# Products with few output rows, dealt out over four groups of 32 output partitions, in a four-layer hybrid trunk

## The chip, the cores and the metric

The kernel runs as one program on 1 core of one Trainium2 chip. The metric is the device time of one execution in microseconds; lower is better. The number compared is the median over several runs.

## The reference, cut to what matters

One inference step of a trunk with four layers of kinds A, B, C, A, on 128 context tokens and 256 latent tokens, model width D = 1024, all in fp32. Each layer first makes its modulation vectors from two conditioning vectors, and its mixer follows. Three parts of it matter here:

```
sc, scc = silu(c), silu(c_ctx)                      # two vectors of 1024
for l in range(4):                                  # kinds A, B, C, A
    mod_p = scc @ w_mod[l] + b_mod[l]               # 1024 x 3072 weights, one row each:
    mod_s = sc  @ w_mod[l] + b_mod[l]               #   two "modulation rows" per layer
    h = rmsnorm(y) * (1 + scale) + shift            # from mod, per sequence
    ...
# kind A (layers 0 and 3): input and forget gates of 4 heads in 2 directions = 16 rows
    gin  = concat([q, k, v])                        # q, k, v: 4x4 blocks of xc, xc, xm (2048 wide)
    ipre = gin @ w_ig + b_ig ;  lf = log_sigmoid(gin @ w_fg + b_fg)
# kind B (layer 1): decay through rank 16, two directions
    la[d] = log_sigmoid((h @ w_a1[d]) @ w_a2[d] + b_a[d]) / 16
```

## The kernel before, in words

Every engine has one instruction list, written out by hand, and the lists meet in semaphores. Activations lie with features on the partitions: `hT` is 8 blocks of 128 features by 385 columns (128 context tokens, a spare column, 256 latent tokens). Nearly every product writes one of two PSUM banks, `acc0` and `acc1`, in a fixed order of tiles that `plan()` numbers. TensorE may write tile n when tile n-2 has been moved out (`acc_moved`), and the mover, mostly ScalarE, waits for `acc_ready`.

All big weights stream through a `ring` of two slots of 2 MB, filled by the SP queue in a fixed order of chunks. A chunk's DMAs are issued when the last tile that reads the chunk two places earlier is done.

**Modulation.** A layer's 3072 modulation columns are made in `MOD_CHUNKS` = 8 parts of `MC` = 384. One part (`mod_part`) is one ring chunk of 1.5 MB and one group of `KD` = 8 products: the stationary operand is a pair of columns of `sc` (the two silu vectors, 128 features of them), the moving one is 128 x 384 of the weights, and the output is 2 x 384. ScalarE moves this to `mst`. `mod_columns` then turns it into columns with three transposes of 2 x 128, and ScalarE moves 6 columns to `modr`. Layer 0's parts run at the start, between the four `fold` steps, which build gate weights on VectorE. The parts of layer l+1 run inside layer l: two per head in layer 0 (`head`: one between the score products and `den`, the other before the products with the state), six between the levels of layer 1's attention and two after it, and one after every second head of layer 2. Layer 3 runs none.

**Gate sums.** In `mlstm` (layers 0 and 3), 32 products with 16 stationary columns (`g4`, in `gfold`, which lies in `kw[0]`) and 385 moving columns sum up into a 16 x 385 tile: 16 of them on `xm`, then 16 on `xc`. ScalarE moves that to `grow`, and two products with the selector `gsel` spread the 16 rows to rows 0 to 3 and 32 to 35 of two tiles.

**The low-rank step.** In `gla` (layer 1), two groups of 8 products with 16 stationary columns (`ga1`), one per direction, write 16 x 385 each. ScalarE moves both to `gha`, and 8 products with `ga2` (16 rows of contraction) follow. GpSimd's queue loads `ga1`, `ga2` and the layer's state when the layer begins.

Each product appears once in the kernel and twice in the trace: the program issues 8 products for a modulation part, and the trace has 16 matmul records, each with its own weight load, in the order in which the products stand.

Of the kernel before, what the change touches and what calls it, by code (L numbers as in the profile page):

```python
# [55 lines left out]
CHUNK = 4096  # L56

# [3 lines left out]
def plan():  # L61
# [12 lines left out]
    for l, kind in enumerate(KINDS):  # L74
        folds = [[(name, l, *counts) for name, *counts in part] for part in fold]
        if l == 0:
            phases += mod(0, 0, 1) + folds[0] + folds[1] + mod(0, 2, 3) + folds[2] + mod(0, 4, 5) + folds[3]
            phases += mod(0, 6, 7) + folds[4]
        phases += [("norm", l, 0, 2)]
        if kind == 0:  # L80
            if l:
                phases += sum(folds, [])
            phases += [("xm", l, 4, 16), ("z", l, 4, 16), ("gate", l, 0, 3), ("pre", l, 0, 12), ("cols", l, 0, 1)]
            for h in range(AH):
                first, second = mod(l + 1, 2 * h), mod(l + 1, 2 * h + 1)

                phases += [(f"first{h}", l, 0, 1)] + first + [(f"c0_{h}", l, 1, 0), (f"state{h}", l, 0, 9)] + second
                phases += [(f"rest{h}", l, 0, 14 if h < AH - 1 else 2)]
            phases += [("out", l, 4, 8)]
        elif kind == 1:  # L90
            phases += [("q", l, 1, 4), ("k", l, 1, 4), ("la", l, 0, 10), ("v", l, 2, 6), ("g", l, 2, 8)]
            phases += [("state", l, 0, 6)] + mod(l + 1, 0, 1, 2, 3, 4, 5) + [("rms", l, 0, 3)] + mod(l + 1, 6, 7)
            phases += [("rms3", l, 0, 1), ("out", l, 2, 8)]
        else:
            phases += [("q", l, 2, 8), ("k", l, 2, 8), ("rmsq", l, 0, 8), ("v", l, 2, 6), ("rmsk", l, 0, 8),
                       ("g", l, 2, 8), ("turn", l, 0, 2), ("knew", l, 0, 2)]
            for k in range(KD):
                phases += [(f"attn{k}", l, 0, 1)] + mod(l + 1, k)
            phases += [("out", l, 2, 8)]
    phases += [("store", 0, 0, 6)]  # L100
    for name, l, chunks, tiles in phases:
        if name in ("xm", "z", "v", "g", "out") or name in ("q", "k") and KINDS[l] == 2:
            assert c % 2 == 0 and t % 2 == 0
# [13 lines left out]
def trunk(nc, i, o):  # L117

    with ExitStack() as ctx:
# [45 lines left out]
        with ExitStack() as st:  # L165
# [7 lines left out]
            kw = [sb(f"kw{d}", ADH, stack=st) for d in range(2)]  # L173
# [31 lines left out]
        g4 = gfold.rearrange("p (f s n) -> p f s n", s=2, n=16)  # L205
# [7 lines left out]
        with ExitStack() as st:  # L213
# [17 lines left out]
            ga2 = sb("ga2", 2 * BH * BDK, rows=RANK, stack=st)  # L231
            gha = sb("gha", 2 * W, rows=RANK, stack=st)
# [38 lines left out]
        const_dve = sem("const_dve")  # L271
        ring_full = [sem(f"ring_full{s}") for s in range(SLOTS)]
# [219 lines left out]
        def _(pe):  # L492
# [88 lines left out]

            def mod_columns(l, n):
                t = tile(f"modrow{n}", l)
                moved(pe, t)
                transposes(tile(f"modcol{n}", l), [
                    (lambda ps, e=e: ps[:, 2 * e:2 * e + 2], mst[:, seg(n % 2 * MC + e * P, P)])
                    for e in range(MC // P)])

            def mod_part(l, n):


                if l == DEPTH:
# [5 lines left out]
                group(ps[0:2, 0:MC], [(sc[:, 2 * k:2 * k + 2], w3[:, k, :]) for k in range(KD)]  # L598
                      ).then_inc(acc_ready, 1)
# [153 lines left out]
            def mlstm(l):  # L753
# [37 lines left out]
            def gla(l):  # L791
# [3 lines left out]
                pe.wait_ge(b_in, 16 * 5)  # L795
# [3 lines left out]
                for d in range(2):  # L799
                    moved(pe, tile("la", l, d))  # L800
                    for h in range(BH):
                        n = d * BH + h
                        mm(bank(tile("la", l, 2 + n))[:, 0:W], ga2[:, n * BDK:(n + 1) * BDK],
                           gha[:, d * W:(d + 1) * W], True, True).then_inc(acc_ready, 1)
# [171 lines left out]
        def _(act):  # L976
# [42 lines left out]
            move(tile("vec", 0, 1), sc.rearrange("p (k r) -> p r k", r=2),  # L1019
# [13 lines left out]
            def mod_part(l, n):  # L1033
# [3 lines left out]
                move(tile(f"modrow{n}", l), mst[:, seg(n % 2 * MC, MC)], lambda ps: ps[0:2, 0:MC])  # L1037
# [83 lines left out]
            def mlstm(l):  # L1121
# [16 lines left out]
                nc.scalar.copy(grow[:, 0:P], ps[0:16, 0:P])  # L1138
                move(tile("gate", l, 0), grow[:, P:TC], lambda ps: ps[0:16, LAT:W])
# [33 lines left out]
            def gla(l):  # L1173
# [4 lines left out]
                for d in range(2):  # L1178
                    move(tile("la", l, d), gha[:, d * W:(d + 1) * W], lambda ps: ps[0:RANK, 0:W])
                for n in range(2 * BH):  # L1180
                    both_sequences(tile("la", l, 2 + n), dx[0][:, n * TC:(n + 1) * TC], bias=vec[:, V_BA + n:V_BA + n + 1])
                moved_all(act, "la", l, 10)
# [127 lines left out]
        def _(dve):  # L1310
# [11 lines left out]
            for t, x in ((vrow[:, :], 0.0), (rowp[:, :], 0.0), (eps[:, :], EPS), (ones[:, :], 1.0),  # L1322
                         (ones_d[:, :], 1.0 / D), (ones_h[:, :], 1.0 / ADH),
                         (y3[:, :, NCTX:LAT], 0.0)):
                ins = nc.vector.memset(t, x)
            ins.then_inc(const_dve, 1)

# [48 lines left out]
            def prepare(l):  # L1376

                done_before(dve, l - 1)
                for t in (xm3[:, :, 0:1], xm3[:, :, W + 1:W + 2], gsel, r_ab[:, :], r_m[:, :]):
                    ins = nc.vector.memset(t, 0.0)  # L1380
                link(ins)
                dve.wait_ge(const_made, CONSTS)
                for x in range(4):
# [4 lines left out]
                nc.vector.tensor_copy(gsel.rearrange("p (n c) -> p n c", c=32)[:, :, 0:AH],  # L1388
                                      ident[0:16, 0:16].rearrange("p (n c) -> p n c", c=AH)).then_inc(gsel_ready, 1)
# [320 lines left out]
        def _(pool):  # L1710
# [57 lines left out]
            def gla(l):  # L1768
                done_before(pool, l - 1)
                for d in range(2):  # L1770
                    pool.dma_start(ga14[:, :, d, :], i["b_w_a1"][0, d].rearrange("(k p) n -> p k n", p=P)).then_inc(b_in, 16)
                    pool.dma_start(ga2[:, seg(d * BH * BDK, BH * BDK)], i["b_w_a2"][0, d]).then_inc(b_in, 16)
# [90 lines left out]
```

## Time and profile before

| what | value |
|---|---|
| time of 3 runs, median (lowest, highest) | 1951.1 us (1944.92, 1952.26) |
| the profiled execution: its own time, first to last instruction | 1948.8 us |
| TensorE busy | 1816.9 us, 93% |
| VectorE, ScalarE, GpSimd busy | 604.2, 495.2, 167.7 us |
| mean granted TensorE clock | 0.968 of 2.4 GHz |
| share of the chain that ended last that is TensorE's | 88% |

Shares are of the span. A line that begins with L500 is the helper `mm` that issues every plain product, and one that begins with L565 is a transpose, so groups are told apart by their tiles (`acc<-ring,sc` is the modulation rows). A matmul's busy time runs from its start to the modelled end, and neighbours overlap: 16 records of 0.486 us each can take 5.32 us together.

### The profile page before, as it was taken

The numbers are of one execution on the slowest core, as the hardware profiler recorded it, in microseconds if no ns is written. First come the engines' busy times: TensorE is split into PE (matmuls) and PEld (weight loads), VectorE is DVE, ScalarE is ACT, GpSimd is POOL, SyncE is SP. The second block draws the span as 40 slices with busy tenths as digits, with TensorE's granted clock in tenths as the row PEclk, the third lists the DMA queues.
The fourth block names the chain that finished last, engine by engine and source line by source line (L and its number), as shares of the span: only waits on it lengthen the run. The fifth ranks groups of instructions, "written<-read, shape, count | busy, mean of one in ns | idle before, by whom it ended". The sixth has DMA issues, their size and how long they took to land.

```text
span 1948.8 us, 16614 instructions
## 1 busy us (share of the span) xinstructions
PE 1816.9 (93%) x6421; PEld 1050.9 (54%) x6421; DVE 604.2 (31%) x979; ACT 495.2 (25%) x960; POOL 167.7 (9%) x158
## 2 busy tenths in 40 slices
PE   6899999999989899988989998999799998898998
PEld 3355534755655554546455455545455536575655
DVE  0333005336340202375320552321433005445420
ACT  2201323323320114343111222231201223433300
POOL 1000001001000000052043000000100001100100
PEclk9999998999999998999999997999899999999999
DMA  6522222233242321242365221323222221212122
GB/s 189 203 86 86 88 74 76 76 112 116 83 146 95 113 86 43 76 150 98 130 126 156 86 86 44 98 98 110 73 86 87 99 74 44 83 48 87 44 88 75
DMA packets 105140, 185.98 MB, mean 95 GB/s; under 512 B 5136, under 2 KB 54704, under 8 KB 105072
## 3 DMA queue, kind: packets, MB, share of 16 engines
q1 hardware_dynamic: 95816, 158.40, 24.2%
q0 software_dynamic: 8640, 26.46, 4.6%
q8 instruction: 49, 0.80, 0.2%
q10 hardware_dynamic: 616, 0.16, 0.1%
q14 instruction: 19, 0.16, 0.0%
HBM read 164.47 MB, written 20.54 MB: 95 GB/s over the span
## 4 chain that ended last, share of the span: by engine, by line
PE 88%; DVE 5%; ACT 3%; issue 1%; DMA 1%; SPq 0%; DVEq 0%; ACTq 0%; POOLq 0%
PE acc L500 69%; PE mix L500 17%; PE acc L565 1%; DMA out_new_C<-cst 1%; DVE hT L1523 1%; ACT cp L1276 1%; DVE mix L1344 1%; DVE rd L1505 1%; DVE cstat L1666 1%; PE mix L915 0%; DMA ring<-in_a_w_out 0%; DMA cst<-in_c_k_g 0%; DVE dx L1590 0%; DVE hT L1348 0%; DVE fqk L1626 0%
## 5 line engine op out<-in xcount | busy, mean ns | idle before, releaser
L500 PE MATMUL acc<-hT,ring 128*128 128x385 f32 x1664 | 548.3, 491 | 15.8 <-DVE hT L1351 14.4
L500 PEld LDWEIGHTS acc<-hT,ring 128*128 128x128 f32 x1664 | 317.9, 192 | 244.6 <-issue 21.9
L500 PE MATMUL acc<-z,ring 128*128 128x385 f32 x512 | 169.5, 492 | 6.1 <-DMA ring<-in_a_w_out 4.2
L500 PE MATMUL acc<-ring,sc 128*2 128x384 f32 x512 | 170.2, 486 | 1.6 <-ACT mst L992 1.2
L500 PEld LDWEIGHTS acc<-z,ring 128*128 128x128 f32 x512 | 97.9, 192 | 77.7 <-issue 6.1
L500 PE MATMUL mix<-qs,ring 128*128 128x256 f32 x512 | 117.6, 392 | 9.6 <-DVE qs L1507 9.6
L500 PEld LDWEIGHTS mix<-qs,ring 128*128 128x128 f32 x512 | 100.1, 197 | 27.6 <-issue 13.2
L500 PEld LDWEIGHTS acc<-ring,sc 128*2 128x2 f32 x512 | 41.3, 85 | 119.1 <-issue 112.2
L1363 DVE SCALAR_TENSOR_TENSOR y<-acc,modv,y 128x128 f32 x64 | 23.4, 413 | 223.8 <-PE acc L500 223.8
L500 PE MATMUL acc<-ring,hT 128*128 128x512 f32 x192 | 85.5, 608 | 0.0
L500 PE MATMUL acc<-xc,bd 128*128 128x385 f32 x128 | 57.5, 574 | 14.2 <-DVE hT L1523 8.4
L500 PE MATMUL acc<-vtok,kw 128*128 128x512 f32 x128 | 61.5, 610 | 5.9 <-ACT cst L992 5.9
L1445 DVE SCALAR_TENSOR_TENSOR pm<-pm,fl 64x384 f32<-64x384 f32 x2 | 1.1, 550 | 207.3 <-ACT fl L1145 207.3
L500 PEld LDWEIGHTS acc<-ring,hT 128*128 128x128 f32 x192 | 37.3, 195 | 48.1 <-issue 48.1
L992 ACT ACTIVATE mst<-acc 2x384 f32<-2x384 f32 x32 | 15.3, 479 | 177.4 <-PE acc L500 177.4
L1523 DVE TENSOR_TENSOR hT<-hT,acc 128x385 f32<-128x385 f32 x32 | 15.6, 551 | 137.5 <-PE acc L500 137.5
L1123 ACT COPY xm<-acc 128x385 f32 x32 | 15.4, 480 | 163.1 <-PE acc L500 163.1
L1757 POOL TENSOR_SCALAR kw<-ktok,cols 128x512 f32<-128x512 f32 x16 | 34.3, 2150 | 250.4 <-ACT ktok L992 238.1
L1047 ACT ACTIVATE hT<-y x24 | 12.6, 525 | 167.6 <-DVE y L1363 167.2
L992 ACT ACTIVATE cst<-acc 128x512 f32<-128x512 f32 x64 | 37.7, 597 | 68.4 <-PE acc L500 55.8
L500 PE MATMUL acc<-hT,ones_h 128*128 128x385 f32 x128 | 44.7, 491 | 9.1 <-ACT hT L1118 9.1
L1666 DVE TENSOR_REDUCE cstat<-mix 128x1 f32<-128x384 f32 (+1 forms) x48 | 19.5, 462 | 98.4 <-PE mix L500 98.4
(297 smaller groups left out, 2212.6 us busy)
## 6 DMA issues: line engine op xcount, KB each, us to landing
ring<-in_w_mod SPq DMA_DIRECT2D x64, 768.0 KB, 6.2
ring<-in_a_w_in SPq DMA_DIRECT2D x32, 1024.0 KB, 6.9
ring<-in_state_mlstm_C SPq DMA_DIRECT2D x16, 1024.0 KB, 7.8
out_new_C<-cst POOLq DMA_DIRECT2D x32, 512.0 KB, 3.2
ring<-in_a_w_out SPq DMA_DIRECT2D x16, 1024.0 KB, 7.8
ring<-in_c_w_in SPq DMA_DIRECT2D x16, 1024.0 KB, 7.6
ring<-in_b_w_in SPq DMA_DIRECT2D x12, 1024.0 KB, 6.3
ring<-in_b_w_out SPq DMA_DIRECT2D x4, 1024.0 KB, 6.2
```

Source lines behind the costliest of these rows:

```text
L500: return nc.tensor.matmul(out, lhsT=lhsT, rhs=rhs, start=start, stop=stop)
L565: ins = nc.tensor.transpose(out(ps), src, ident[0:src.shape[0], 0:src.shape[0]])
L992: nc.scalar.activation(out, src(ready(n)), func, **kw_).then_inc(acc_moved[n % 2], 1)
L1047: nc.scalar.activation(hT[:, bass.ds(it * (2 * W) + e * W, W)], y[:, bass.ds(it * (2 * W) + e * W, W)], ACT.Square).then_inc(sq_ready, 1)
L1123: pair_loop(tile("xm", l), AT_, lambda it, e, ps: nc.scalar.copy(xm[:, bass.ds(it * (2 * (W + 2)) + (e * (W + 2) + 1), W)], ps[:, 0:W]))
L1276: ins = nc.scalar.activation(cp[s][:, seg(c, n)], mix[:, seg(q * 512, n)], ACT.Exp, bias=cst_[s][:, q:q + 1], accum_out=cst_[s][:, 3 + q:4 ...
L1344: link(nc.vector.reciprocal(inv, rstd[:, :]))
L1363: ins = stt(yc, ps[:, seg(c, n)], modv[:, bass.ds(it * 4 + (2 * (2 * KD + e) + r), 1)], yc, ALU.mult, ALU.add)
L1505: link(nc.vector.reciprocal(rd[d][:, :], rd[d][:, :]))
L1523: tt(h3[:, e, :], h3[:, e, :], acc[t % 2][:, 0:W], ALU.subtract).then_inc(cen_ready if e < HT - 1 else acc_moved[t % 2], 1)
L1666: ins = nc.vector.tensor_reduce(st_[:, q:q + 1], mix[:, seg(q * 512, n)], AX, ALU.max)
L1757: nc.gpsimd.tensor_scalar(kw[d][:, :], ktok[:, :], cols[:, seg(192 + 32 * d + h, 1)], None, ALU.mult).then_inc(kw_ready, 1)
```

## The change

Every group of products with 2 or 16 output rows now goes to four groups of 32 output partitions. Product n writes partitions 32j to 32j+31 with j = n mod 4, so four partial sums stand in one bank, and the products that follow add them.

- The modulation products take 32 columns of `sc` in place of 2: the pair, and 30 of the columns behind it, whose rows nobody reads. `mst` has 128 rows. `mod_columns` has three full products with a selector `sel` (128 x 2, a one in row p and column r where p mod 32 = r) in place of three transposes.
- The gate products take 32 columns of `gfold` (16 of them zero); `gfold` is cleared each time and lies in both halves of `kw`, `gsel` and `grow` in `qs`, and `gsel` has its rows four times.
- The low-rank step takes both directions at once (32 columns): 8 products in place of 16 and one move in place of two. `ga2` is cleared on GpSimd and loaded four times over, in 8 DMAs in place of 2.

```diff
-        sc = sb("sc", 2 * KD)
+        sc = sb("sc", 2 * KD + GRP - 2)
+        sel = sb("sel", 2)
-        mst = sb("mst", 2 * MC, rows=2)
+        mst = sb("mst", 2 * MC)
-        gfold = kw[0]
-        grow = kw[1][0:16, 0:TC]
+        gfold = kw_both
+        grow = qs[0][:, 0:TC]
+            def packed(ps, width, n, a, b, first, last):
+
+                j = n % NG
+                return mm(ps[j * GRP:(j + 1) * GRP, 0:width], a, b, first, last)
...
-                transposes(tile(f"modcol{n}", l), [
-                    (lambda ps, e=e: ps[:, 2 * e:2 * e + 2], mst[:, seg(n % 2 * MC + e * P, P)])
-                    for e in range(MC // P)])
+                for e in range(MC // P):
+                    ins = mm(ps[:, 2 * e:2 * e + 2], mst[:, seg(n % 2 * MC + e * P, P)], sel[:, :], True, True)
+                ins.then_inc(acc_ready, 1)
...
-                group(ps[0:2, 0:MC], [(sc[:, 2 * k:2 * k + 2], w3[:, k, :]) for k in range(KD)]
-                      ).then_inc(acc_ready, 1)
+                for k in range(KD):
+                    ins = packed(ps, MC, k, sc[:, 2 * k:2 * k + GRP], w3[:, k, :], k < NG, k >= KD - NG)
+                ins.then_inc(acc_ready, 1)
...
-                    ins = mm(ps[0:16, 0:W], a, b, n == 0, n == len(pairs) - 1)
+                    ins = packed(ps, W, n, a, b, n < NG, n >= len(pairs) - NG)
...
-                for d in range(2):
-                    group(bank(tile("la", l, d))[0:RANK, 0:W], [(ga14[:, k, d, :], h3[:, k, :]) for k in range(KD)]
-                          ).then_inc(acc_ready, 1)
+                for k in range(KD):
+                    ins = packed(ps, W, k, ga1[:, k * GRP:(k + 1) * GRP], h3[:, k, :], k < NG, k >= KD - NG)
...
-                for t in (xm3[:, :, 0:1], xm3[:, :, W + 1:W + 2], gsel, r_ab[:, :], r_m[:, :]):
+                for t in (xm3[:, :, 0:1], xm3[:, :, W + 1:W + 2], gsel, gfold, r_ab[:, :], r_m[:, :]):
...
+                nc.gpsimd.memset(ga2[:, :], 0.0).then_inc(ga2_zero, 1)
...
+                    for g in range(NG):
+                        pool.dma_start(ga2[seg(g * GRP + d * RANK, RANK), seg(d * BH * BDK, BH * BDK)], i["b_w_a2"][0, d]
+                                       ).then_inc(b_in, 16)
```

On TensorE, around layer 0's gate sums (`acc<-xm,kw` and `acc<-xc,kw`), the list before reads:

```order
L500 MATMUL acc<-xm,kw 16x385 x16
L500 MATMUL acc<-xc,kw 16x385 x16
L500 MATMUL acc<-kw 64x384 x2
L500 MATMUL acc<-xc,bd 128x385 x8
L500 MATMUL acc<-bd,xm 128x128 x12
```

And now:

```order
L506 MATMUL acc<-xm,kw 32x385 x16
L506 MATMUL acc<-xc,kw 32x385 x16
L506 MATMUL acc<-qs 64x384 x2
L506 MATMUL acc<-xc,bd 128x385 x8
L506 MATMUL acc<-bd,xm 128x128 x12
```

Nothing moved: the counts are the same, the outputs have 32 rows, and the selector is read from `qs`.

On TensorE, in layer 0's first head, from the products for the denominators' first part (`acc<-aq,vec`) to the products with the stored state (`mix<-qs,ring`), before:

```order
L500 MATMUL acc<-aq,vec 128x256 x8
L500 MATMUL acc<-ring,sc 2x384 x8
L500 MATMUL mix<-pm,ones 128x128
L500 MATMUL mix<-pm,ones 128x256 x2
L500 MATMUL mix<-pm,ones 128x128
L500 MATMUL mix<-pm,ones 128x256 x2
L500 MATMUL acc<-vtok,kw 128x512 x8
L500 MATMUL acc<-ktok,cols 2x512
L500 MATMUL acc<-ring,sc 2x384 x8
L565 MATMUL acc<-ident,mst 128x2 x3
L500 MATMUL mix<-qs,ring 128x256 x32
```

And now:

```order
L506 MATMUL acc<-aq,vec 128x256 x8
L506 MATMUL acc<-ring,sc 32x384 x8
L506 MATMUL mix<-pm,ones 128x128
L506 MATMUL mix<-pm,ones 128x256 x2
L506 MATMUL mix<-pm,ones 128x128
L506 MATMUL mix<-pm,ones 128x256 x2
L506 MATMUL acc<-vtok,kw 128x512 x8
L506 MATMUL acc<-ktok,cols 2x512
L506 MATMUL acc<-ring,sc 32x384 x8
L506 MATMUL acc<-sel,mst 128x2 x3
L506 MATMUL mix<-qs,ring 128x256 x32
```

Again nothing moved: the modulation products write 32 rows, and the three transposes have become three products.

On GpSimd, the loads at the start of layer 1 (`ga` is both `ga1` and `ga2`), before:

```order
L1771 DMA ga<-in_b_w_a 128x8x16
L1772 DMA ga<-in_b_w_a 16x512
L1771 DMA ga<-in_b_w_a 128x8x16
L1772 DMA ga<-in_b_w_a 16x512
L1773 DMA gs<-in_state_gla_S 128x8x256
L1774 IOTA gxor 128x128
L1775 IOTA gxs 128x128
```

And now:

```order
L1789 MEMSET ga 128x1024
L1791 DMA ga<-in_b_w_a 128x8x16 x2
L1795 DMA ga<-in_b_w_a 16x512 x8
L1797 DMA gs<-in_state_gla_S 128x8x256
L1798 IOTA gxor 128x128
L1799 IOTA gxs 128x128
```

The memset and six more DMAs stand ahead of the state's DMA and of the two iotas.

## Rows read from the trace of the kernel before

**Rows 1.** The page: span, busy time by engine, the last chain by engine.

```profile
span 1948.8 us, 16614 instructions
PE 1816.9 (93%) x6421; PEld 1050.9 (54%) x6421; DVE 604.2 (31%) x979; ACT 495.2 (25%) x960; POOL 167.7 (9%) x158
...
PE 88%; DVE 5%; ACT 3%; issue 1%; DMA 1%; SPq 0%; DVEq 0%; ACTq 0%; POOLq 0%
```

**Rows 2.** TensorE's groups by shape: count, busy us, mean ns, idle us ahead.

```profile
L500 PE MATMUL acc<-ring,sc 128*2 128x384 f32 x512 | 170.2, 486 | 1.6 <-ACT mst L992 1.2 <-DVE rd L1401 0.4
...
L500 PE MATMUL acc<-xc,kw 128*16 128x385 f32 x64 | 21.1, 486 | 0.0
L500 PE MATMUL acc<-xm,kw 128*16 128x385 f32 x64 | 21.1, 487 | 0.0
...
L500 PE MATMUL acc<-hT,ga 128*16 128x385 f32 x32 | 10.5, 486 | 0.0
```

**Rows 3.** Timeline of TensorE, layer 0's first head: start us, length us.

```profile
297.24 3.00 PE L500 MATMUL acc<-bd,xm 128*128 128x128 f32 x24
...
318.20 5.32 PE L500 MATMUL acc<-ring,sc 128*2 128x384 f32 x16
323.45 2.44 PE L500 MATMUL mix<-pm,ones 128*128 128x128 f32 x12
...
340.80 0.34 PE L565 MATMUL acc<-ident,mst 2*128 2x2 f32 x3
```

**Rows 4.** The tile mst: its transposes, min, median and max ns.

```profile
L565 PE MATMUL acc<-ident,mst x96: 189/196/219, 31.0 to 1337.1; 2*128 2x2 f32 x96
```

**Rows 5.** Timeline of TensorE at the start, layer 0's modulation parts.

```profile
39.75 5.43 PE L500 MATMUL acc<-ring,sc 128*2 128x384 f32 x16
...
45.74 5.32 PE L500 MATMUL acc<-ring,sc 128*2 128x384 f32 x16 [0.30 <-ACT mst L992]
...
83.05 5.49 PE L500 MATMUL acc<-hT,ones_d 128*128 128x256 f32 x32 [1.19 <-issue]
```

**Rows 6.** DMA from 20 to 80 us: rate in 40 slices, us to landing.

```profile
GB/s 5 0 0 0 25 230 401 372 143 363 400 163 0 11 0 0 0 45 315 398 290 34 321 399 290 5 29 229 397 384 38 217 397 376 30 0 164 404 388 396
...
ring<-in_w_mod SPq DMA_DIRECT2D x12, 768.0 KB, 5.6
```

**Rows 7.** Timeline of VectorE in layer 0's first head, ahead of the denominators.

```profile
318.31 0.75 DVE L1483 TENSOR_TENSOR rd<-wi,acc 128x256 f32<-128x256 f32 x2 [7.54 <-PE acc L500]
...
320.24 0.41 DVE L1489 TENSOR_TENSOR pm<-pm,mix 128x256 f32<-128x256 f32 x1
```

**Rows 8.** Layer 1's level loop, 841 to 905 us: each engine's busy us, PEclk.

```profile
841.00:905.00 64.00, 55.94 (x306) 30.87 (x304) 53.72 (x26) 24.56 (x37) 34.49 (x7) 1.00 0.51 164
```

**Rows 9.** The same loop: the chain that ended last.

```profile
873.80 5.25 PE acc L500 x16
...
882.20 5.25 PE acc L500 x16
...
887.73 1.49 issue
889.22 2.92 PE mix L500 x24
```

**Rows 10.** The same loop: timelines of ScalarE and GpSimd.

```profile
887.49 0.48 ACT L992 ACTIVATE mst<-acc 2x384 f32<-2x384 f32 x1 [4.63 <-PE acc L500]
...
882.94 6.17 POOL L1784 TENSOR_TENSOR fqk<-fqk,gk 128x1536 f32<-128x1536 f32 x1 [5.59 <-ACT fqk L1211]
```

**Rows 11.** Layer 2, one modulation part: timelines of TensorE and ScalarE.

```profile
1213.90 5.32 PE L500 MATMUL acc<-ring,sc 128*2 128x384 f32 x16
1219.15 0.92 PE L500 MATMUL mix<-ck,cq 64*128 64x128 f32 x4
...
1214.27 0.20 ACT L1276 ACTIVATION_READ_ACCUMULATOR cp<-mix,cstat 128x1 f32 x1
```

**Rows 12.** Layer 1's start: timelines of GpSimd and TensorE.

```profile
671.47 0.90 POOL L1773 DMA_DIRECT2D gs<-in_state_gla_S  x1
...
722.08 10.54 PE L500 MATMUL acc<-hT,ga 128*16 128x385 f32 x32
```

**Rows 13.** A memset's length, and TensorE's wait in layer 3's fold.

```profile
0.97 0.48 DVE L1325 MEMSET cst<- 128x512 f32 x1 [0.97 <-PEq L1852]
...
1397.94 5.13 PE L500 MATMUL acc<-z 128*128 128x256 f32 x12 [1.92 <-DVE z L1384]
```

More of the change, by code:

```diff
@@ L56 @@
 CHUNK = 4096
+GRP = 32
+NG = P // GRP
 def plan():
@@ L102, in plan @@
         if name in ("xm", "z", "v", "g", "out") or name in ("q", "k") and KINDS[l] == 2:
-            assert c % 2 == 0 and t % 2 == 0
+            assert c % 2 == 0
         chunk0[name, l], tile0[name, l] = c, t
@@ L172, in trunk @@
             ktok = sb("ktok", ADH, stack=st)
-            kw = [sb(f"kw{d}", ADH, stack=st) for d in range(2)]
+            kw_both = sb("kw", 2 * ADH, stack=st)
             bd = sb("bd", 3 * HT * P, stack=st)
@@ L191, in trunk @@
         nst = r_ab[0:2, 0:ADH]
-        gfold = kw[0]
-        grow = kw[1][0:16, 0:TC]
-        gsel = kw[1][0:16, TC:TC + P]
+        kw = [kw_both[:, d * ADH:(d + 1) * ADH] for d in range(2)]
+        gfold = kw_both
+        grow = qs[0][:, 0:TC]
+        gsel = qs[0][:, TC:TC + P]
         vrow = cst[0][:, 0:4 * P]
@@ L204, in trunk @@
         bd4 = bd.rearrange("p (m e c) -> p m e c", m=3, e=HT)
-        g4 = gfold.rearrange("p (f s n) -> p f s n", s=2, n=16)
+        g4 = gfold.rearrange("p (f s n) -> p f s n", s=2, n=GRP)
         qs3 = [v3(t, HT, NLAT) for t in qs]
@@ L793, in gla @@
                 linear("k", l, 1, KD, 4, h3, W)
-                pe.wait_ge(b_in, 16 * 5)
-                for d in range(2):
-                    group(bank(tile("la", l, d))[0:RANK, 0:W], [(ga14[:, k, d, :], h3[:, k, :]) for k in range(KD)]
-                          ).then_inc(acc_ready, 1)
[L799 to L804, printed above, removed]
+                pe.wait_ge(b_in, 16 * 11)
+                ps = bank(tile("la", l, 0))
+                for k in range(KD):
+                    ins = packed(ps, W, k, ga1[:, k * GRP:(k + 1) * GRP], h3[:, k, :], k < NG, k >= KD - NG)
+                ins.then_inc(acc_ready, 1)
+                moved(pe, tile("la", l, 0))
+                for n in range(2 * BH):
+                    mm(bank(tile("la", l, 1 + n))[:, 0:W], ga2[:, n * BDK:(n + 1) * BDK], gha[:, :], True, True
+                       ).then_inc(acc_ready, 1)
                 linear("v", l, 2, KD, 4, h3, W, tokens=True)
@@ L1036, in mod_part @@
                     return
-                move(tile(f"modrow{n}", l), mst[:, seg(n % 2 * MC, MC)], lambda ps: ps[0:2, 0:MC])
+                move(tile(f"modrow{n}", l), mst[:, seg(n % 2 * MC, MC)], lambda ps: ps[:, 0:MC])
                 for m in range(max(n - 1, 0), n + (n == MOD_CHUNKS - 1)):
@@ L1137, in mlstm @@
                 ps = ready(tile("gate", l, 0))
-                nc.scalar.copy(grow[:, 0:P], ps[0:16, 0:P])
-                move(tile("gate", l, 0), grow[:, P:TC], lambda ps: ps[0:16, LAT:W])
+                nc.scalar.copy(grow[:, 0:P], ps[:, 0:P])
+                move(tile("gate", l, 0), grow[:, P:TC], lambda ps: ps[:, LAT:W])
                 move(tile("gate", l, 1), r_ig, lambda ps: ps[0:64, 0:TC], ACT.Identity, bias=rowp[:, ia:ia + 1])
@@ L1177, in gla @@
                     both_sequences(tile("k", l, h), gk3[:, h, :])
-                for d in range(2):
-                    move(tile("la", l, d), gha[:, d * W:(d + 1) * W], lambda ps: ps[0:RANK, 0:W])
+                move(tile("la", l, 0), gha[:, :], lambda ps: ps[:, 0:W])
                 for n in range(2 * BH):
-                    both_sequences(tile("la", l, 2 + n), dx[0][:, n * TC:(n + 1) * TC], bias=vec[:, V_BA + n:V_BA + n + 1])
-                moved_all(act, "la", l, 10)
+                    both_sequences(tile("la", l, 1 + n), dx[0][:, n * TC:(n + 1) * TC], bias=vec[:, V_BA + n:V_BA + n + 1])
+                moved_all(act, "la", l, 9)
                 link(nc.scalar.activation(dx[1][:, :], dx[0][:, :], ACT.Abs))
@@ L1323, in _ @@
                          (ones_d[:, :], 1.0 / D), (ones_h[:, :], 1.0 / ADH),
-                         (y3[:, :, NCTX:LAT], 0.0)):
+                         (y3[:, :, NCTX:LAT], 0.0), (sc[:, :], 0.0)):
                 ins = nc.vector.memset(t, x)
             ins.then_inc(const_dve, 1)
+            dve.wait_ge(const_made, CONSTS)
+            nc.vector.tensor_reduce(sel[:, :], ident.rearrange("p (j r) -> p r j", r=GRP)[:, 0:2, :], AX, ALU.add
+                                    ).then_inc(sel_ready, 1)
             def mod_vectors(l):
```

28 lines of the change are left out of this document (18 added, 10 removed).

## The prediction

> **What bounds the kernel now.** I read the page first: TensorE is busy 93% of a span of 1948.8 us, and 88% of the chain that ended last is TensorE's [rows 1]. So a product that gets shorter counts nearly in full, unless it covers somebody else's work. Then the groups by shape, for what the change touches: the modulation rows take 170.2 us (512 records, 32 parts of 16), the gate sums 21.1 + 21.1 us over two layers, the low-rank step's first half 10.5 us [rows 2]. That is 222.9 us. The reader should see that the mean of one record is 486 or 487 ns in all four groups, whether 2 or 16 output rows are written, and that 16 of them take 5.32 us [rows 3]. So records start (5.32 - 0.486)/15 = 0.322 us apart: the 384 or 385 moving columns set the pace, and the output rows don't. Last I read the places where modulation parts stand between other engines' work: the start, the heads, the level loop of layer 1, and layer 2.
>
> **The dealt groups.** The program keeps the same number of products (16 fewer records in the low-rank step). Whether products for different groups of 32 output rows run at the same time is the whole question, and no row before shows two groups side by side. If they don't, a record still starts 0.322 us after the last; if four do, four start in that time. What I take lies between, for this reason: a product is two records, both for the same rows, and records stand in the trace in the order of the list. The second record of a product needs the rows that the first still streams through, so it starts 0.322 us later; the next product's first record stands behind it in the list, and can start with it, not before. So two run at a time, and n products take n steps and the last record's 0.486 us.
>
> The Trainium skill (TensorE: Matmul & The Clock Gate, Part 3, The mechanism) says that matmuls start and end in program order, and that weight loads alone are pulled ahead. By that rule the two at a time stand, and with them the sum below. The same part of that page (Measured speedup vs the span model) has three column tiles of 32 at 2.38 times; by that alone a part would take 5.32/2.38 = 2.24 us and the kernel, by the same sum, about 1845 us, which is an estimate from that page; no run here shows such tiles yet.
>
> A step is 0.322 us plus the time d between two starts that don't wait for each other. d lies between 0 and the closest starts I find, the three transposes: 0.34 us in all, the last 0.196, so (0.34 - 0.196)/2 = 0.072 us apart [rows 3, 4]. I take 0.03, under the middle, as a transpose's start also loads 128 stationary columns, and these load 32.
>
> **A modulation part**: 8 x 0.352 + 0.486 = 3.30 us in place of 5.32, a gain of 2.02. Against it, three products with `sel` replace three transposes of 0.34 us. They have 128 stationary columns and 2 moving ones and are six records; 24 records of 128 by 128 take 3.00 us [rows 3], 0.12 apart, so six take about 0.72: a loss of 0.38, between 0 (as before) and 0.54 (0.12 x 5 + a full record of 0.278). Net 1.64 us a part.
>
> Of the 32 parts, 26 stand where TensorE has no other wait to fall back on, if their covers hold:
> - Layer 0's eight, at the start. Six parts and other work lie between 39.75 and 83.05 us [rows 5]; 6 x 5.66 are parts, 9.3 the rest. After: 6 x 4.02 + 9.3 = 33.4 us, 5.6 a chunk. A chunk of 1.57 MB takes 3.9 us at the 400 GB/s that the rate reaches, and 5.6 us from issue to landing [rows 6]. That is just hidden.
> - Eight in layer 0's heads. The first part of a head covers VectorE's scaling of the scores: that ends at 320.24 + 0.41 = 320.65 [rows 7], 2.45 us after the part's start [rows 3]. 3.30 us still cover it. Behind the second part only shared shifts follow.
> - Eight in layer 2. The part covers the exponentials that the next scores wait for; they end at 1214.47, 0.57 us into it [rows 11].
> - Two after layer 1's attention, with nothing beside them.
>
> 26 x 1.64 = 42.6 us.
>
> The other six stand in layer 1's level loop, and there VectorE is busy for 53.7 of 64 us, nearly as long as TensorE [rows 8]. In the loop's second half the last chain does run through parts [rows 9], because ScalarE waits for a part's end before it makes the next factors, and GpSimd's 6.17 us product follows those [rows 10]. A shorter part brings that forward until VectorE or GpSimd is late instead, which the "issue" piece of 1.49 us already shows. Three parts on the chain would give 4.9 us; I take 3.5, between 1 and 4.9.
>
> **Gate sums**: 32 x 0.352 + 0.486 = 11.75 us a layer, 23.5 for both in place of 42.2: 18.7 us. What waits for them (ScalarE, then VectorE's rows) moves forward with them.
>
> **Low-rank step**: 8 products in place of 16, so 3.30 in place of 10.54 us: 7.2 us. Its loads grow by a memset and six DMAs ahead of the state's. The state's DMA was issued at 671.47, each issue takes at most 0.9 us, and the step starts at 722.08 [rows 12]; with ten more microseconds of queue (six issues and the memset) and a landing like that of a ring chunk (5.6 us, [rows 6]), over 30 us are left. So nothing; if the cover were gone, some 10 us.
>
> **Clearing `gfold`**: 128 x 1024, twice the 0.48 us of a 128 x 512 memset [rows 13]. In layer 0 it runs while TensorE makes the first two parts, ahead of any fold product. In layer 3 TensorE waits for the VectorE copies right behind it [rows 13], so 1.0 us is lost.
>
> **Sum**: 42.6 + 3.5 + 18.7 + 7.2 - 1.0 = 71.0 us. 1948.8 - 71.0 = 1877.8. The runs shown have a median of 1951.1, 2.3 us over the profiled span, so I add that: **1880 us**. With d = 0, the columns at no loss and the loop at 4.9 this case gives 58.8 + 4.9 + 20.6 + 7.5 - 1.0 = 90.8, so 1860; with d = 0.072, the columns at 0.54 and the loop at 1 it gives 29.6 + 1 + 16.0 + 6.9 - 1.0 = 52.5, so 1899.
>
> **Rivals.**
>
> *Four at a time.* The second record of a product doesn't hold up the next product. For it: nothing in a row forbids it. Against it: in all rows records start in list order. A part then takes 3 x 0.322 + 0.486, about 1.5 us, net 3.44, but covers give out: at the start six chunks need 23.4 us of DMA against 22.6 us of work, and the landing shows too (3.5 us in all); each head's first part leaves 1.0 us of VectorE's 2.45 open (4 us). 26 x 3.44 - 7.5 = 82; loop 4.9; gates 42.2 - 2 x 5.3 = 31.6; low rank 9.0; less 1.0: 126.5, so **1825 us**. The Trainium skill (TensorEngine Tiling, Theoretical Speedup) allows up to 4 times for 32 columns.
>
> *No overlap at all*, so the change doesn't do what it says: the step stays 0.322 us whatever the rows. For it: one pace for 2 and for 16 rows [rows 2]. Then the selector products cost 26 x 0.38 = 9.9 and 1 in the loop, the memset 1.0, and the low-rank step still halves (-5.2): +6.7, so **1958 us**.
>
> *Slower.* A change of group makes a record wait until the one before is written out: 0.486 between starts and not 0.322, 0.164 more. That falls on 7 changes a part and 31 in a gate sum: 26 x (1.15 + 0.38) + 5.5 in the loop + 2 x 5.1 - 4.1 + 1.0 = 52, so **2003 us**. It decides early: with no overlap, 0.012 us a change (251 changes) is enough for 0.5% slower. The Trainium skill (TensorEngine Tiling, Key Properties) says that changing the tiling mode drains the array, and not changing the tile; by that rule this rival's price is not paid. No row here shows a change of group.
>
> **Chances.** Two at a time 0.58, four 0.20, no overlap 0.12, slower 0.10. About 0.5% (10 us) is what a measurement of this kernel can tell from no change. So faster 0.78, same 0.12, slower 0.10. The likeliest case has 1860 to 1899 by itself; with four at a time the range is 1818 to 1900, and the other two are left out.
>
> **What would show it.** In the changed trace, 16 `acc<-ring,sc` records in about 3.3 us, starting in twos about 0.35 us apart, each still 0.48 us long; the gate's 64 in 11.8; six `acc<-sel,mst` records in 0.7; TensorE waiting on nothing new at the start; VectorE as busy as before in layer 1's loop, now without TensorE beside it. It is wrong if the records run one or four at a time, if the parts' covers were thinner than I read them, or if TensorE's granted clock, 1.00 in that loop now [rows 8], falls to 1.2 GHz there once TensorE pauses between levels: a level's products of 2.92 us [rows 9] and a part would then take some 13 us together, and the loop would give back up to 24 us.

## The result, and the profile after

The changed kernel takes 1830.54 us (median of 4 runs, 1827.67 to 1837.2), beside 1951.27 us before (4 runs, 1944.92 to 1952.26): a ratio of 0.9395, 95% interval 0.9371 to 0.942, so 121 us less. The forecast was 1880 us, with 1818 to 1900 as the range. The time lies inside the range, but not where the likeliest case had it (1860 to 1899): the case of four at a time, which had a chance of 0.20, gave 1825.

The page of the changed kernel, with the span, TensorE's share and the last chain's shares, answers to [rows 1]:

```profile
span 1825.9 us, 16809 instructions
PE 1672.0 (92%) x6501; PEld 1033.8 (57%) x6501; DVE 608.4 (33%) x989; ACT 497.9 (27%) x959; POOL 172.1 (9%) x165
...
PE 84%; DVE 7%; ACT 3%; DMA 3%; issue 2%; ACTq 0%; SPq 0%; DVEq 0%; POOLq 0%
```

TensorE still bounds the kernel. What shrank is seen in its groups by shape, against [rows 2]:

```profile
L506 PE MATMUL acc<-ring,sc 128*32 128x384 f32 x512 | 49.6, 506 | 5.3 <-DMA ring<-in_w_mod 5.3
...
L506 PE MATMUL acc<-xm,kw 128*32 128x385 f32 x64 | 5.6, 490 | 0.0
L506 PE MATMUL acc<-xc,kw 128*32 128x385 f32 x64 | 5.5, 487 | 0.0
...
L506 PE MATMUL acc<-hT,ga 128*32 128x385 f32 x16 | 1.5, 493 | 0.0
```

The mean of one record is as before (486 to 506 ns), and the counts of the first three groups too. But 170.2 us became 49.6, and 42.2 became 11.1: the records of different groups lie on top of one another. How many at a time is read from the timeline of TensorE's products (start, length, count) at layer 0's gate sum and in its first head:

```profile
241.45 2.79 PE L506 MATMUL acc<-xm,kw 128*32 128x385 f32 x32
244.06 2.77 PE L506 MATMUL acc<-xc,kw 128*32 128x385 f32 x32
...
281.06 1.50 PE L506 MATMUL acc<-ring,sc 128*32 128x384 f32 x16
282.77 2.44 PE L506 MATMUL mix<-pm,ones 128*128 128x128 f32 x12 [0.21 <-DVE pm L1508]
```

and from that of its weight loads in the same part:

```profile
281.06 0.16 PEld L506 LDWEIGHTS acc<-ring,sc 128*32 128x32 f32 x8 [0.33 <-issue]
281.41 0.13 PEld L506 LDWEIGHTS acc<-ring,sc 128*32 128x32 f32 x4 [0.19 <-issue]
...
```

A part of 16 records takes 1.50 us where it took 5.32 [rows 3]: four rounds of four records each, 0.322 to 0.35 us apart. The loads show it plainly: eight at once (for each of the four groups the first record and, behind it, its second), then four with each round. The 64 records of a gate sum go the same way, 5.4 us in all.

Where the 122.9 us between the two profiled executions lie, from the starts of TensorE's first record of each stage in the two timelines (us; the differences are taken before rounding):

| stage | before | after | difference | forecast |
|---|---|---|---|---|
| start, to layer 0's norm (8 parts) | 83.0 | 61.7 | -21.3 | -13.1 |
| two gate sums | 43.2 | 12.2 | -30.9 | -18.7 |
| layer 0's heads to the low-rank step (8 parts) | 414.6 | 386.9 | -27.7 | -13.1 |
| low-rank step | 19.2 | 9.2 | -10.1 | -7.2 |
| layer 1's `v` and `g` to its loop | 98.0 | 94.9 | -3.1 | 0 |
| level loop (6 parts) | 68.2 | 65.6 | -2.6 | -3.5 |
| loop's end to `out` (2 parts) | 35.9 | 31.7 | -4.2 | -3.3 |
| layer 2 (8 parts) | 394.4 | 370.1 | -24.3 | -13.1 |
| layer 3's norm to its gate sum (`gfold` cleared) | 195.1 | 196.2 | +1.2 | +1.0 |
| all else | 597.3 | 597.4 | +0.2 | 0 |

A part outside the loop gains 3.82 us, and its columns (the products with `sel`) lose some 0.42: from their start to that of the next product it is 0.69 us in the first head (296.27 to 296.96), where it was 0.27 (340.80 to 341.07). That is 3.40 net. 26 of them would be 88.4; the four stages with parts show 77.5. The view of TensorE's waits names most of the rest, three waits for ring chunks that weren't there before, 5.3 + 2.1 + 1.7 = 9.1 us:

```profile
PE acc L506 <- DMA ring<-in_w_mod: 5.3, 3, 2.7
...
PE acc L506 <- DMA ring<-in_c_w_out: 2.1, 1, 2.1
PE acc L506 <- DMA ring<-in_b_w_out: 1.7, 1, 1.7
```

They stand where longer parts covered a transfer; for the two `out` weights this is read from the place alone, and no run tried it. At the start (timeline, against [rows 5]) the parts wait for their own weights:

```profile
41.76 1.50 PE L506 MATMUL acc<-ring,sc 128*32 128x384 f32 x16 [2.75 <-DMA ring<-in_w_mod]
...
45.94 1.81 PE L506 MATMUL acc<-ring,sc 128*32 128x384 f32 x16 [1.92 <-DMA ring<-in_w_mod]
...
61.72 5.49 PE L506 MATMUL acc<-hT,ones_d 128*128 128x256 f32 x32 [1.19 <-issue]
```

Behind the second of these waits a part takes 1.81 us and not 1.50: from 20 to 62 us the granted clock has a mean of 0.84, where before it had 0.96. In a second trace of the changed kernel (`e9_after_again`) the clock is 0.92 there, the three waits of 5.3 us are four of 7.3, and the norm starts at 60.87.

The level loop hardly moved, though TensorE lost most of six parts there. A level's products need two factors: VectorE makes one (its `fqk` product) and GpSimd the other. The loop's window of 64 us (busy us of each engine, then the granted clock), and VectorE's, GpSimd's and TensorE's timelines in it, against [rows 8 to 10]:

```profile
763.20:827.20 64.00, 41.54 (x321) 34.22 (x320) 55.88 (x27) 25.43 (x37) 35.19 (x7) 0.82 0.50 165
```

```profile
767.92 4.99 DVE L1645 TENSOR_TENSOR fqk<-fqk,gq 128x1536 f32<-128x1536 f32 x1
...
786.26 1.75 DVE L1645 TENSOR_TENSOR fqk<-fqk,gq 128x1536 f32<-128x1536 f32 x1
```

```profile
766.63 4.66 POOL L1808 TENSOR_TENSOR fqk<-fqk,gk 128x1536 f32<-128x1536 f32 x1 [7.05 <-ACT fqk L1224]
...
783.45 7.87 POOL L1808 TENSOR_TENSOR fqk<-fqk,gk 128x1536 f32<-128x1536 f32 x1 [7.23 <-ACT fqk L1224]
...
801.79 7.91 POOL L1808 TENSOR_TENSOR fqk<-fqk,gk 128x1536 f32<-128x1536 f32 x1 [5.55 <-ACT fqk L1224]
```

```profile
761.47 4.63 PE L506 MATMUL mix<-fqk 128*128 128x128 f32 x40
...
772.97 5.07 PE L506 MATMUL mix<-fqk 128*128 128x128 f32 x24 [5.44 <-DVE fqk L1645]
...
781.22 2.94 PE L506 MATMUL mix<-fqk 128*128 128x128 f32 x24 [1.00 <-DVE fqk L1645]
...
791.41 4.39 PE L506 MATMUL mix<-fqk 128*128 128x128 f32 x24 [5.06 <-issue]
...
809.80 5.39 PE L506 MATMUL mix<-fqk 128*128 128x128 f32 x24 [5.10 <-issue]
...
827.12 2.05 PE L506 MATMUL mix<-dx,gs 128*128 128x256 f32 x4 [4.28 <-DVE dx L1652]
```

VectorE is busy 55.9 of 64 us now, TensorE 41.5 where it was 55.9. TensorE waits 5 us three times. The first wait, until 772.97, is for VectorE, whose product ends at 767.92 + 4.99 = 772.91. The other two, until 791.41 and 809.80, have no releaser in the view ("issue"), but GpSimd's product for the same level ends right before each: 783.45 + 7.87 = 791.32 and 801.79 + 7.91 = 809.70, while VectorE's was ready earlier (786.26 + 1.75 = 788.01 for the first). So these two are for GpSimd. The level products behind the three waits take 5.07, 4.39 and 5.39 us and not 2.94: the granted clock falls, in the last of them to 1.2 GHz, as a window on it shows (span, products, weight loads, the other engines, clock):

```profile
809.80:815.10 5.30, 5.30 (x24) 5.16 (x24) 1.52 (x1) 0.00 (x0) 4.82 (x1) 0.51 0.05 18
```

### The profile page after: what moved, and what is told of

Same layout as the page of the kernel before. It is cut to its first block, busy times and chain, and to the rows that moved or that the text cites. A ratio compares the mean times of both kernels' runs of the same rounds, so it can differ in the third digit from the quotient of the medians.

```text
span 1825.9 us, 16809 instructions
## 1 busy us (share of the span) xinstructions
PE 1672.0 (92%) x6501; PEld 1033.8 (57%) x6501; DVE 608.4 (33%) x989; ACT 497.9 (27%) x959; POOL 172.1 (9%) x165
## 4 chain that ended last, share of the span: by engine, by line
PE 84%; DVE 7%; ACT 3%; DMA 3%; issue 2%; ACTq 0%; SPq 0%; DVEq 0%; POOLq 0%
PE acc L506 65%; PE mix L506 18%; DMA ring<-in_w_mod 1%; DVE dx L1609 1%; DMA out_new_C<-cst 1%; PE acc L571 1%; DVE hT L1542 1%; DVE fqk L1645 1%; ACT cp L1289 1%; DVE mix L1360 1%; DVE rd L1524 1%; DVE cstat L1685 1%; DMA ring<-in_c_w_out 0%; PE mix L929 0%; DMA ring<-in_a_w_out 0%
## 5 line engine op out<-in xcount | busy, mean ns | idle before, releaser
L1379 DVE SCALAR_TENSOR_TENSOR y<-acc,modv,y 128x128 f32 x64 | 23.4, 413 | 223.2 <-PE acc L506 223.2
L506 PE MATMUL acc<-ring,sc 128*32 128x384 f32 x512 | 49.6, 506 | 5.3 <-DMA ring<-in_w_mod 5.3
L1444 DVE TENSOR_SCALAR xc<-xm,vec x32 | 15.4, 481 | 104.4 <-ACT xm L1137 104.4
L506 PEld LDWEIGHTS acc<-xc,bd 128*128 128x128 f32 x128 | 23.7, 203 | 45.3 <-ACT aq L1006 13.6
L1678 DVE RECIPROCAL cqr<-cqr 128x385 f32<-128x385 f32 x8 | 20.5, 2557 | 82.3 <-ACT cqr L1006 82.3
```

Source lines behind the costliest of these rows:

```text
L506: return nc.tensor.matmul(out, lhsT=lhsT, rhs=rhs, start=start, stop=stop)
L1379: ins = stt(yc, ps[:, seg(c, n)], modv[:, bass.ds(it * 4 + (2 * (2 * KD + e) + r), 1)], yc, ALU.mult, ALU.add)
L1678: link(nc.vector.reciprocal(r3[:, k, :], r3[:, k, :]))
```

## Experiments

**1. Blocks in place of turns** (`e1_blocks`). The same products, as many to each group, but each group gets its share in one block.

```diff
-                j = n % NG
-                return mm(ps[j * GRP:(j + 1) * GRP, 0:width], a, b, first, last)
+                q = total // NG
+                j = n // q
+                return mm(ps[j * GRP:(j + 1) * GRP, 0:width], a, b, n % q == 0, n % q == q - 1)
```

> Same products, same sums, same four groups of output partitions, but dealt out in blocks: the first quarter of a step's products goes to group 0, the next to group 1, and so on (two and two in a modulation part, eight and eight in a gate sum), so that products that follow one another share a group. Theory A, each group has a queue of its own that takes all records of its block: the four groups still run side by side, a part stays at 1.50 us, a gate sum at 5.4 us, and the span at 1826 us. Theory B, a group takes one record and holds one more, and the list stands still behind a third: a group's block lets the next one begin only when its last record but one has started, so a part takes 3.2 to 3.4 us and a gate sum near 19 us, and the span is near 1890 us. Theory C, the prediction's own step (a record starts only when the record ahead of it in the list has started): a part takes 4.2 to 4.4 us, a gate sum near 20 us, the span near 1915 us.

Measured: 1856.03 us, ratio 0.9519 (0.9482 to 0.9556), span 1858.2. No theory holds alone. A part keeps its 1.5 us, as A has it; the gate's stage (from its first record to the next product) grows from 6.1 to 17.8 us, near B. The timelines of products (the gate sum's last records, and one part) and of weight loads (the gate sum's first block):

```profile
257.96 8.29 PE L506 MATMUL acc<-xc,kw 128*32 128x385 f32 x29
...
300.53 1.52 PE L506 MATMUL acc<-ring,sc 128*32 128x384 f32 x16
```

```profile
249.13 0.14 PEld L506 LDWEIGHTS acc<-xm,kw 128*32 128x32 f32 x2 [0.55 <-issue]
249.48 0.11 PEld L506 LDWEIGHTS acc<-xm,kw 128*32 128x32 f32 x1 [0.21 <-issue]
...
252.72 0.11 PEld L506 LDWEIGHTS acc<-xm,kw 128*32 128x32 f32 x1 [0.21 <-issue]
253.04 0.14 PEld L506 LDWEIGHTS acc<-xm,kw 128*32 128x32 f32 x3 [0.21 <-issue]
```

From 249.13 to 252.72 one group alone loads 13 times (2, then 11 by one). At 253.04 three loads fall together: the first group's 14th of 16, and the first two of the second group. So the list went on to the next group when two records of the first still stood unloaded. C, the prediction's step, falls in a part (1.52 us, not 4.2 to 4.4); what holds the list up is a third record for a group that has two waiting. The gate sum lasts from 249.13 to 257.96 + 8.29 = 266.25, 17.1 us. The two waiting records must be counted for each group by itself: one limit of two for all groups together would put a part in blocks of two products at 2.1 us (an estimate, worked out with starts 0.322 us apart in a group), and it takes 1.52.

Of the 32.3 us by which the span grew against the changed kernel, the two gate stages are 23.4. Another 4.4 lie in the start, where the granted clock has a mean of 0.71 from 20 to 62 us (0.84 in the changed kernel).

**2. Turns of four in the gate sum** (`e7_gate_fours`), to try that number where it gives another answer.

```diff
-                    ins = packed(ps, W, n, a, b, n < NG, n >= len(pairs) - NG)
+                    j = n // 4 % NG
+                    ins = mm(ps[j * GRP:(j + 1) * GRP, 0:W], a, b, n < 16 and n % 4 == 0, n >= 16 and n % 4 == 3)
```

> As the changed kernel, but the 32 gate products go to the groups in turns of four (8 records in a row to a group), where the changed kernel gives one product at a time and e1_blocks eight. Theory: a group takes the record that runs, one whose weights are loaded and a fixed number of records behind these; the list stands still at the next. With two records held behind (as the 13th start in a block of e1_blocks says, where the next group began), the 64 records take 12.0 us from the first start to the last end; with one held 14.3 us, with three 9.8 us; with no limit 5.4 us; one record at a time 20.8 us. The stage of the gate is then near 13 us, against 6.1 in the changed kernel and 17.8 in e1_blocks.

Measured: span 1843.5 us; the profiled execution is the only one. The gate sum's timeline:

```profile
241.88 5.78 PE L506 MATMUL acc<-xm,kw 128*32 128x385 f32 x29
...
248.17 5.76 PE L506 MATMUL acc<-xc,kw 128*32 128x385 f32 x29
```

From 241.88 to 248.17 + 5.76 = 253.93 are 12.05 us. Two held back give 12.0, one 14.3, three 9.8, as worked out before the run: two it is.

**3. One group and two** (`e3_one_group`, `e4_two_groups`): `NG` is 1 or 2, and what follows reads 32 or 64 rows.

```diff
-NG = P // GRP
+NG = 1
...
-                    ins = mm(ps[:, 2 * e:2 * e + 2], mst[:, seg(n % 2 * MC + e * P, P)], sel[:, :], True, True)
+                    ins = mm(ps[:, 2 * e:2 * e + 2], mst[0:NG * GRP, seg(n % 2 * MC + e * P, P)], sel[0:NG * GRP, :], True, True)
```

> Everything of the change but the dealing: all products of the three steps go to the first 32 rows, and what follows reads 32 rows. A part should take 16 records of 0.322 us and a tail, 5.3 us, as before. If the dealing alone is what saves: against before, the columns by sel cost +0.38 us for 26 exposed parts (+9.9) and the joint low-rank step saves 8 products in 2 records of 0.322 us (-5.2): span 1953 us, ratio 1.00. If the other edits save by themselves (the columns as products, fewer tiles), the span is under 1935 us.

> Two groups of 32 rows in place of four. If the groups run independently, each with 8 records of 0.322 us in a part: 2.6 us and a tail, 2.75 us a part, 10.5 us a gate sum, 2.75 us for the low-rank step; against the changed kernel +1.25 us for some 18 to 24 parts that nothing covers (+22 to +30), +5.2 us for each gate sum (+10), +1.25 for the low-rank step: span 1860 to 1867 us. If the step holds (a record starts only when the one ahead of it in the list has started, two at a time whatever the number of groups), a part takes 2.9 us, and four groups would not have been any better than two.

Measured: one group 1959.93 us, ratio 1.0061 (1.0041 to 1.0082), span 1957.0; two groups 1866.7 us, ratio 0.9582 (0.9552 to 0.9612), span 1865.7. A part and half a gate sum with one group, then the same with two:

```profile
263.91 10.54 PE L506 MATMUL acc<-xm,kw 128*32 128x385 f32 x32
...
319.91 5.35 PE L506 MATMUL acc<-ring,sc 128*32 128x384 f32 x16
```

```profile
250.04 5.37 PE L506 MATMUL acc<-xm,kw 128*32 128x385 f32 x32
...
297.41 2.77 PE L506 MATMUL acc<-ring,sc 128*32 128x384 f32 x16
```

So 5.35, 2.77 and 1.50 us for one, two and four groups: 16, 8 and 4 rounds that start 0.322 us apart, and the last record's 0.486 us. Without the dealing, the rest of the change costs 8 us by the spans (1957.0 against 1948.8) and 0.6%, some 12 us, by the ratio of the times. All of the gain is the dealing's.

**4. Modulation parts alone** (`e2_mods_only`).

```diff
-                    ins = packed(ps, W, n, a, b, n < NG, n >= len(pairs) - NG)
+                    ins = mm(ps[0:GRP, 0:W], a, b, n == 0, n == len(pairs) - 1)
...
-                    ins = packed(ps, W, k, ga1[:, k * GRP:(k + 1) * GRP], h3[:, k, :], k < NG, k >= KD - NG)
+                    ins = mm(ps[0:GRP, 0:W], ga1[:, k * GRP:(k + 1) * GRP], h3[:, k, :], k == 0, k == KD - 1)
```

> Only the modulation parts are dealt out; the 32 gate products and the 8 products of the low-rank step all go to the first 32 rows (the low-rank step still for both directions at once). If the savings add up as the stages of the changed kernel's trace show them: gate sums back from 5.4 us to about 20.8 us, twice, so +31 us; low-rank step from 1.5 to 5.3 us, +3.8 us; span 1861 us. If a later wait takes over what the gates gain (the other theory), the span is under 1850 us.

Measured: 1867.1 us, ratio 0.9587 (0.9552 to 0.9621), span 1865.1, against 1861 by the sum. The gate stages went back to 21.6 us each (+31.0), the low-rank step from 9.2 to 14.0 (+4.8), `v` and `g` from 94.9 to 96.9. The savings add up, and no later wait takes over what the gates gain.

**5. The loop's parts undealt** (`e5_loop_undealt`): parts 0 to 5 of layer 2 to the first 32 rows.

```diff
+                    if part_rows(l, n) == GRP:
+                        ins = mm(ps[0:GRP, 0:MC], sc[:, 2 * k:2 * k + GRP], w3[:, k, :], k == 0, k == KD - 1)
...
```

> Of the parts, only the six of layer 2 that lie in layer 1's loop (0 to 5) go back to the first 32 rows; all else as in the changed kernel. Theory A, that loop is bound by VectorE and GpSimd and TensorE waits there: the loop goes from 65.7 us back to about 68 us, the span from 1825.9 to 1828 or 1829 us. Theory B, TensorE's own work sets the loop's length: 6 times 3.8 us, +23 us, span 1849 us.

Measured: 1838.42 us, ratio 0.9429 (0.9402 to 0.9455), span 1836.7. A holds for the loop, as TensorE's timeline there shows:

```profile
765.50 4.63 PE L511 MATMUL mix<-fqk 128*128 128x128 f32 x40
770.06 5.35 PE L511 MATMUL acc<-ring,sc 128*32 128x384 f32 x16
...
834.19 2.05 PE L511 MATMUL mix<-dx,gs 128*128 128x256 f32 x4 [4.28 <-DVE dx L1662]
```

From 765.50 to 834.19 are 68.7 us, +3.0 against 65.6, for 23 us more of products. The span grew by 10.8, more than A said. 3.8 of it lie in the stage of layer 0's heads (390.7 for 386.9), 1.7 from layer 1's `out` products to layer 2's norm (45.15 for 43.45) and 1.7 in layer 3 up to its gate sum (197.9 for 196.2). In these stages the two programs are the same, so I don't put them down to this edit: the heads' stage lies between 386.6 and 391.6 in the five other traces of kernels that share it.

**6. Layer 0's weights earlier** (`e6_start`, `e8_start_later`, and the changed kernel beside them as `e9_after_again`). Chunks 2 to 5 get places of their own, so their transfers wait for no ring slot; `e8_start_later` issues them only when the small constants have landed.

```diff
+        early = dict(zip(EARLY, (xm[:, 0:KD * MC], xm[:, KD * MC:2 * KD * MC], xc[:, KD * MC:2 * KD * MC], hT[:, 0:KD * MC])))
...
+                if l == 0 and n in EARLY:
+                    if n == EARLY[0]:
+                        sp.wait_ge(vec_in, 16 * VECTORS)
+                    src = i["w_mod"][l].rearrange("(k p) n -> p k n", p=P)[:, :, n * MC:(n + 1) * MC]
+                    dst = early[n].rearrange("p (k n) -> p k n", k=KD)
+                    for k in (slice(0, KD // 2), slice(KD // 2, KD)):
+                        sp.dma_start(dst[:, k], src[:, k]).then_inc(early_in[n], 16)
...
```

(The two lines with the wait are those of `e8_start_later`; VectorE's clearing of the edges of `xm` moves behind the parts in both.)

> The changed kernel with layer 0's modulation weights 2 to 5 loaded into four places of their own (xm, xc and hT, which nothing uses then), so that their transfers start at once and don't wait for a slot of the ring. Theory A, the start is now held up by transfers that wait for a slot: TensorE's waits for them there (2.75 + 1.92 + 0.63 us) go, and the stretches at the low granted clock shrink; layer 0's norm starts 5 to 9 us earlier than at 61.7 us, span 1817 to 1821 us. Theory B, the transfers' own rate (near 380 GB/s) binds: the weights arrive no earlier in sum, the start is within 2 us of 61.7 us, span 1824 to 1828 us.

> e6_start with one more wait: the four early transfers of modulation weights are issued only when the small constants have landed, which came 1.8 us later in e6_start (TensorE's first product at 15.10 us there, 13.27 in the changed kernel). If the early transfers were what held the constants up, the first product is back near 13.3 us and layer 0's norm starts at 54.0 to 54.5 us, 1.5 to 2 us before e6_start and 7.5 us before the changed kernel: span 1817 to 1820 us. If the later transfers now come late for parts 2 to 5, TensorE waits for them again and the norm starts at 56 us or later.

> The changed kernel itself, beside e8_start_later on the same chip: 1826 to 1832 us, ratio 0.937 to 0.942. If e8_start_later saves what its start says, its ratio is lower by 0.003 to 0.005.

Measured: 1822.99 us, ratio 0.9359 (0.9342 to 0.9376); 1821.66, 0.9344 (0.9332 to 0.9357); and 1830.27, 0.9392 (0.9377 to 0.9406) for the changed kernel on the second one's chip. `e6_start`'s timeline at the start, and `e8_start_later`'s, each with TensorE's first product and the norm:

```profile
15.10 1.30 PE L579 MATMUL acc<-ident,cst 128*128 128x128 f32 x5 [15.10 <-DMA cst<-in_c]
...
55.96 5.49 PE L514 MATMUL acc<-hT,ones_d 128*128 128x256 f32 x32 [1.19 <-issue]
```

```profile
14.10 1.30 PE L581 MATMUL acc<-ident,cst 128*128 128x128 f32 x5 [14.10 <-DMA cst<-in_c]
...
55.94 5.49 PE L516 MATMUL acc<-hT,ones_d 128*128 128x256 f32 x32 [1.18 <-issue]
```

Theory A holds for `e6_start`: no wait for modulation weights is left, and the norm starts at 55.96 in place of 61.72. The start was held up by slots, not by the transfers' rate. The later issue brought TensorE's first product forward by 1.0 us and the norm by nothing, so that expectation falls: the first early part then takes 2.65 us (granted clock 0.53) where `e6_start` has 2.03 (0.72), and the next one starts at 37.01 and 37.03. Against the changed kernel on the same chip the better start is 0.5% faster (8.6 us by the medians). In the start 5.8 us show against the changed kernel's first trace and 4.9 against the one on the same chip, whose norm starts at 60.87; the rest is no more than what profiled executions differ by.

## Why the prediction was right and wrong

**What held.** That the whole question is whether groups run side by side, and that the gain then counts nearly in full: 77.5 of 88.4 us for the parts, all of it for the gate sums. The time lies in the range only because the range took in the rival; the sum that gave 1880 had its main term wrong.

**The step that failed** is the one on the dealt groups: "The second record of a product needs the rows that the first still streams through, so it starts 0.322 us later; the next product's first record stands behind it in the list, and can start with it, not before. So two run at a time". The first half is right (a group's records are 0.322 us apart). The second isn't: priced at 3.30 us, a part took 1.50; a record that waits for its group steps aside, and up to two of them may. In turns of one product the list stands still only when all four groups are equally full, so four ran at a time. `e1_blocks` shows the stepping aside by itself: four records in a row go to one group there, and the next groups don't wait for them.

The step also rested on a misreading: "no row before shows two groups side by side" and "in all rows records start in list order". One place in the trace of the kernel before speaks against both, with groups of 64 rows. In layer 2 an even head's value products write output partitions 0 to 63 and an odd head's 64 to 127, and for the last two heads, 14 and 15, they stand next to each other in the list: six records `acc<-cpt,cv` and two `acc<-cpt,cvc` for head 14, then the same for head 15. TensorE's timeline there:

```profile
1328.32 1.39 PE L500 MATMUL acc<-cpt,cv 128*64 128x128 f32 x7
1329.45 0.38 PE L500 MATMUL acc<-cpt,cvc 128*64 128x256 f32 x1
1329.55 0.49 PE L500 MATMUL acc<-cpt,cv 128*64 128x128 f32 x2
1329.67 0.38 PE L500 MATMUL acc<-cpt,cvc 128*64 128x256 f32 x1
```

In list order six `cv` records would come first and both of head 14's `cvc` behind them. The trace has seven before the first `cvc` and two more before the second: three records of head 15 started ahead of one of head 14 that stands before them in the list, and beside others of head 14. This was evidence for the rival, and it went into no chance.

The Trainium skill (TensorE: Matmul & The Clock Gate, Part 3, The mechanism) had the same order, matmuls start in program order; these runs differ: a part's second record stands ahead of the third to eighth in the list and starts 0.322 us after its first, and 16 records in 1.50 us leave no room unless the other groups' first records start before it. That page's 2.38 for three column tiles (Measured speedup vs the span model) lies between what is measured here for two groups, 5.32/2.77 = 1.92, and for four, 5.32/1.50 = 3.55.

**The terms.**
- Parts: priced at 3.30 us, measured 1.50. Columns at +0.38, measured +0.42. 26 x 1.64 = 42.6 forecast, 77.5 measured.
- d, the time between free starts, was put at 0.03 us and hardly shows: three steps of 0.322 us and the last record's 0.486 make 1.45 of the 1.50 us.
- Gate sums: 11.75 us a layer forecast, 5.4 measured; 18.7 became 30.9.
- Low-rank step: 3.30 forecast, 1.50 measured; the stage gave 10.1, not 7.2. Its longer queue of loads cost nothing, as said. Another 3.1 us came in `v` and `g`; the joint step alone gives 1.2 of them (96.8 with one group), and the cause of the rest is open.
- Loop: 3.5 forecast, 2.6 measured, for the reason given: VectorE is late instead once, GpSimd twice.
- `gfold`: 1.0 forecast; TensorE's wait in layer 3 grew from 1.92 [rows 13] to 3.04:

```profile
1290.14 7.07 PE L506 MATMUL acc<-z 128*128 128x256 f32 x16 [3.04 <-DVE z L1400]
```

**The rivals.** Four at a time was the case that came: 1825 priced for the median, 1830.54 measured. That it comes so near is in part luck, as its terms were off both ways. At the start 5.3 us of transfers showed, where 3.5 were priced. In each of four heads 1.0 us was priced for VectorE's scaling, and TensorE waits 0.21 in the first head alone. The loop gave 2.6 and not 4.9. Two waits for layer 1's and layer 2's `out` weights (1.7 and 2.1 us) were in no case. No overlap is what `e3_one_group` runs: 1958 priced, 1959.93 measured; beside the kernel before on its own chip (1946.82) that is 13 us more, where 6.7 were priced. Slower had changes of group that cost 0.164 us each; a part with its 7 changes takes 1.50 us in all.

**The warning on the clock** came in part: 0.82 in the loop, where it was 1.00 [rows 8]. The products of the three slow levels took 2.1, 1.45 and 2.45 us longer. The chain that ended last runs over VectorE where the first two of them run; only the third is in it itself:

```profile
772.91 1.67 DVE gat L1622
...
792.86 4.99 DVE dx L1609
...
809.80 5.39 PE mix L506 x24
```

So some 2.45 us were given back, not 24.

## What to carry to other kernels

Products with 32 output rows or fewer are worth dealing over the four groups, one product to each in turn: 3.55 times here. The order counts too, since a third waiting record of one group stops the list for all (in fp32, with two records a product, two products in a row to a group are free, four are not). Then look at what the long products covered: here transfers that wait for a slot came out, and a place of their own for four chunks gave 5 to 6 us back. And before you write that no row shows a thing, look for the one place where it could show: here a single spot in the trace, where two products in a row write different partitions, spoke for the rival.

## What the runs showed of the hardware

- Records for different groups of 32 output partitions run side by side, ahead of list order, and each group keeps its own pace of 0.322 us (384 or 385 columns, 1.00 granted): 5.35, 2.77 and 1.50 us for 16 records over one, two and four groups.
- A group holds the record that runs, one that is loaded, and two behind it; the next one for it stops the list. Gate sums of 64 records took 5.4, 12.05 and 17.1 us in turns of two, eight and sixteen records.
- VectorE's products of 128 x 1536 in layer 1 (`dx` and `fqk`) take 1.73 to 1.75 us, in all eleven traces, where no product of GpSimd runs beside them; beside one they take 1.73 to 5.00. Where VectorE's `fqk` took 4.99, GpSimd's product beside it took 4.66; where VectorE's took 1.75, GpSimd's took 7.87. Which of the two gives way, and when, was not tried; with TensorE's parts short, the loop's length rests on it.
